# A hybrid attention and SSD layer on eight cores: the prologue's tables moved into a unit of their own, and the row copies one iteration later

## What is computed

```
proj = x @ w_in
q, k, v, f_logit, z_att, z_ssd, xbc, dt_raw = split(proj)
log_f = log_sigmoid(f_logit + b_forget);  F = cumsum(log_f)          # per head, over tokens
att = softmax(q.k / sqrt(128) + F[t] - F[s], causal) @ v * silu(z_att)
xbc = silu(causal_depthwise_conv(xbc, conv_w, conv_b))               # 4 taps
dt = softplus(dt_raw + dt_bias);  a_cs = cumsum(dt * A)              # within chunks of 128 tokens
m = (C.B^T) * exp(a_cs[l] - a_cs[s]);  y = m @ (x * dt) + C.state * exp(a_cs) + d_skip * x
state <- state * exp(a_cs[end]) + B^T @ (x * dt * exp(a_cs[end] - a_cs))
y = group_rmsnorm(y * silu(z_ssd)) * ssd_norm_w
out = layer_norm(alpha * x + concat[att, y] @ w_out)
```

## Time and profile before

| | us |
|---|---|
| median of 3 runs (lowest, highest) | 1702.08 (1698.3, 1717.66) |
| profiled execution, its time | 1711.28 |
| its span on the slowest core (core 1) | 1709.7 |
| spans of the eight cores | 1682.9 to 1709.7 |
| DVE, ACT, POOL busy in the span | 1138.4, 857.6, 866.2 |

### The profile page before, as it was taken

How to read it: one execution, slowest core, us unless ns; L and a number is a source line. 1 busy time by engine, 2 the same in 40 slices (tenths; PEclk the granted TensorE clock), 3 DMA queues, 4 the chain that set the end, 5 groups by cost and what they waited for, 6 DMA issues and landing times.

```text
span 1709.7 us, 31962 instructions; the slowest of 8 cores (1682.9 to 1709.7 us)
## 1 busy us (share of the span) xinstructions
PE 1644.7 (96%) x9108; PEld 803.3 (47%) x9108; DVE 1138.4 (67%) x2341; ACT 857.6 (50%) x1979; POOL 866.2 (51%) x1379
## 2 busy tenths in 40 slices
PE   6999889999999999999999999999899999999997
PEld 2444445554454445544544454454445544444443
DVE  2567657777776887787768677767677665444444
ACT  2767656665566666666665665666566620000000
POOL 3265555655565666565655555556566533222221
PEclk9999989999999999999999999999999999999999
DMA  9976783382248224522642373139465876544421
GB/s 150 152 102 118 120 124 86 78 145 63 56 86 131 63 70 98 116 71 63 123 82 64 75 131 71 54 75 141 98 122 113 185 197 199 138 139 136 135 93 74
DMA packets 180218, 185.30 MB, mean 108 GB/s; under 512 B 118668, under 2 KB 136844, under 8 KB 175820
## 3 DMA queue, kind: packets, MB, share of 16 engines
q1 hardware_dynamic: 162620, 120.07, 29.3%
q0 software_dynamic: 17424, 63.18, 23.3%
HBM read 193.50 MB, written 34.60 MB: 133 GB/s over the span
## 4 chain that ended last, share of the span: by engine, by line
PE 84%; DMA 10%; issue 2%; DVE 1%; ACT 1%; POOL 1%; SPq 0%; DVEq 0%; ACTq 0%; another core or an unknown queue 0%; POOLq 0%
PE bank L536 84%; DMA rowb<-arowd 4%; DMA btok<-BT 3%; DMA xq<-xT 3%; DMA slab<-w_out 1%; DMA xtok<-xsf 0%; ACT L547 0%; DVE acc L569 0%; ACT dec L547 0%; POOL xq L597 0%; POOL slab L597 0%; DVE BT L569 0%; DVE xt L569 0%; DVE xsf L569 0%; SPq L595 0%
## 5 line engine op out<-in xcount | busy, mean ns | idle before, releaser
L536 PE MATMUL bank<-xq,slab 128*128 128x512 bf16 x3072 | 731.8, 381 | 5.3 <-DMA slab<-wpack 2.7
L536 PE MATMUL bank<-slab,xq 128*128 128x512 bf16 x2048 | 482.1, 380 | 0.6 <-DMA slab<-wpack 0.6
L536 PEld LDWEIGHTS bank<-xq,slab 128*128 128x128 bf16 x3072 | 293.3, 98 | 312.5 <-issue 15.2
L569 DVE SCALAR_TENSOR_TENSOR acc<-u,cst,acc 128x512 f32<-128x512 f32 x384 | 317.6, 832 | 40.0 <-ACT acc L547 18.5
L536 PEld LDWEIGHTS bank<-slab,xq 128*128 128x128 bf16 x2048 | 198.3, 98 | 215.0 <-issue 3.2
L547 ACT ACTIVATE dec<-rowb,nb 128x128 bf16<-128x128 f32 x512 | 201.8, 397 | 48.5 <-PE bank L536 26.6
L547 ACT ACT_TABLE_LOAD x18 | 23.1, 1283 | 316.5 <-DVE mv L1135 308.7
L547 ACT ACTIVATE P<-bank,boff 128x512 bf16<-128x512 f32 x192 | 131.2, 683 | 78.0 <-PE bank L536 76.8
L536 PE MATMUL bank<-wo,mTa 128*128 128x512 bf16 x704 | 163.4, 379 | 0.0
L558 POOL TENSOR_TENSOR xdd<-xtok,dtde 128x256 bf16<-128x256 bf16 x120 | 82.9, 693 | 128.7 <-PE bank L536 85.9
L569 DVE SCALAR_TENSOR_TENSOR xt<-xt,bank 128x512 f32<-128x512 f32 x64 | 43.8, 685 | 138.5 <-PE bank L536 138.3
(11 more groups left out here) (108 smaller groups left out, 2245.6 us busy)
## 6 DMA issues: line engine op xcount, KB each, us to landing
slab<-wpack POOLq DMA_DIRECT2D x80, 512.0 KB, 7.4
rowb<-arowd SPq DMA_DIRECT2D x128, 256.0 KB, 3.5
xt<-x_tok SPq DMA_DIRECT2D x16, 1024.0 KB, 5.6
out<-xt SPq DMA_DIRECT2D x15, 1024.0 KB, 4.0
xq<-xT POOLq DMA_DIRECT2D x16, 512.0 KB, 26.5
gbc<-growd SPq DMA_DIRECT2D x32, 256.0 KB, 4.1
mixd<-yn SPq DMA_DIRECT2D x128, 64.0 KB, 2.0
slab<-w_out POOLq DMA_DIRECT2D x13, 512.0 KB, 10.4
```

Of the source, the lines that this page charges most:

```text
L536: fns.append(lambda e, o=o, a=a, b=b, s=s, t=t: e.matmul(o, a, b, start=s, stop=t))
L569: return p.op("dve", [lambda e: e.scalar_tensor_tensor(out=o, in0=a, scalar=s, in1=b, op0=op0, op1=op1)], dve_us(n, nptr) + (0.12 if nptr ...
```

## The change

The table part of `prologue_quarter` becomes a function of its own, `prologue_tables`, and a unit of its own, "tab". It is registered behind xs1 of the same step (behind xs1 of quarter 0 and behind B of quarter 1 in the opening list), takes no due time of its own, and its transposes and its matmul write two banks of the projection rotation instead of `PV0` and `PV1`. Iteration 1 reads the one copy of the rows, as iteration 0 does, and the row copies are made in iteration 1, behind the store of its attention output.

```diff
     def copies(i, q):
-        return (slice(0, 1), [1, 128, 512], b_row1[q]) if i == 0 else (slice(0, 16), [16, 8, 512], b_row[q])
+        return (slice(0, 1), [1, 128, 512], b_row1[q]) if i < 2 else (slice(0, 16), [16, 8, 512], b_row[q])
...
+    def prologue_tables(q, t):
+        sp_, e_, cs = [x[:, :] for x in tmps]
+        bs, be, bc = b_pt
+        pr = t - 40
+        B1 = PROJ[pi[0] % 3]
+        B2 = PROJ[(pi[0] + 1) % 3]
+        pi[0] += 2
         lst = []
...
-            fns.append(lambda e, c=c, o=o, src=src: e.transpose(banks[PV0][:, c * 128 + o:c * 128 + o + 64],
+            fns.append(lambda e, c=c, o=o, src=src: e.transpose(banks[B1][:, c * 128 + o:c * 128 + o + 64],
                                                                 src[:, c * 128:(c + 1) * 128], idn[0:64, 0:64]))
-        p.op("pe", fns, 0.6, [bc, bs, b_idn], [bkb[PV0]], pr, tail=0.2)
-        CPY("dve", tokt[:, :, :].rearrange("p a b -> p (a b)"), banks[PV0][:, :], 512, [bkb[PV0]], [b_tokt], pr)
-        MMS([(banks[PV1][:, 0:256], idn[:, 128:256], tokt[:, :, 0:64], True, True, 256, True)], [b_tokt, b_idn],
-            [bkb[PV1]], pr)
+        p.op("pe", fns, 0.6, [bc, bs, b_idn], [bkb[B1]], pr, tail=0.2)
+        CPY("dve", tokt[:, :, :].rearrange("p a b -> p (a b)"), banks[B1][:, :], 512, [bkb[B1]], [b_tokt], pr)
+        MMS([(banks[B2][:, 0:256], idn[:, 128:256], tokt[:, :, 0:64], True, True, 256, True)], [b_tokt, b_idn],
+            [bkb[B2]], pr)
...
-    first = [("fdt", 0), ("k", 0), ("xs0", 0), ("q", 0), ("xs1", 0), ("k", 1), ("xs0", 1), ("q", 1), ("fdt", 1),
-             ("xs1", 1), ("B", 0), ("B", 1), ("C", 0), ("C", 1)]
+    first = [("fdt", 0), ("k", 0), ("xs0", 0), ("q", 0), ("xs1", 0), ("tab", 0), ("k", 1), ("xs0", 1), ("q", 1),
+             ("fdt", 1), ("xs1", 1), ("B", 0), ("B", 1), ("tab", 1), ("C", 0), ("C", 1)]
...
-        do_unit(kind, q, 0, q, due())
+        do_unit(kind, q, 0, q, due() if kind != "tab" else T[0])
...
-                kinds = ["fdt"] + kinds
+                kinds = ["fdt"] + kinds[:4] + ["tab"] + kinds[4:]
...
-                t = due()
+                t = due() if kind != "tab" else T[0]
...
-        if i == 0:
-            copy_rows(q, T[0] + 40, b_mix_att[0][q])
+        if i == 1:
+            copy_rows(q, T[0] + 40, b_mix_att[1][q])
```

More of the change, by code:

```diff
@@ L732, in prologue_quarter @@
         for (c, o, src) in lst:
-            fns.append(lambda e, c=c, o=o, src=src: e.transpose(banks[PV0][:, c * 128 + o:c * 128 + o + 64],
+            fns.append(lambda e, c=c, o=o, src=src: e.transpose(banks[B1][:, c * 128 + o:c * 128 + o + 64],
                                                                 src[:, c * 128:(c + 1) * 128], idn[0:64, 0:64]))
-        p.op("pe", fns, 0.6, [bc, bs, b_idn], [bkb[PV0]], pr, tail=0.2)
-        CPY("dve", tokt[:, :, :].rearrange("p a b -> p (a b)"), banks[PV0][:, :], 512, [bkb[PV0]], [b_tokt], pr)
-        MMS([(banks[PV1][:, 0:256], idn[:, 128:256], tokt[:, :, 0:64], True, True, 256, True)], [b_tokt, b_idn],
-            [bkb[PV1]], pr)
-        ae = banks[PV1][:, 0:256].rearrange("p (c w) -> p c w", w=64)
+        p.op("pe", fns, 0.6, [bc, bs, b_idn], [bkb[B1]], pr, tail=0.2)
+        CPY("dve", tokt[:, :, :].rearrange("p a b -> p (a b)"), banks[B1][:, :], 512, [bkb[B1]], [b_tokt], pr)
+        MMS([(banks[B2][:, 0:256], idn[:, 128:256], tokt[:, :, 0:64], True, True, 256, True)], [b_tokt, b_idn],
+            [bkb[B2]], pr)
+        ae = banks[B2][:, 0:256].rearrange("p (c w) -> p c w", w=64)
         cs_ = slice(4 * q, 4 * q + 4)
@@ L744, in prologue_quarter @@
         CPY("dve", G_tok[:, cs_, :], tokt[:, :, 0:8], 32, [b_tokt], [bt], pr)
-        ACT(cd[:, cs_, :], ae[:, :, 32:64], AF.Exp, 128, [bkb[PV1]], [bt], pr)
+        ACT(cd[:, cs_, :], ae[:, :, 32:64], AF.Exp, 128, [bkb[B2]], [bt], pr)
         if q < 3:
-            CPY("dve", gref[:, q + 1, :], ae[:, 3, 0:8], 8, [bkb[PV1]], [b_tab[q + 1]], pr)
-        TT("dve", tmp2[:, :, :], ae[:, :, 32:64], at_, ALU.subtract, 128, [bkb[PV1], b_tokt], [b_tmp2], pr)
+            CPY("dve", gref[:, q + 1, :], ae[:, 3, 0:8], 8, [bkb[B2]], [b_tab[q + 1]], pr)
+        TT("dve", tmp2[:, :, :], ae[:, :, 32:64], at_, ALU.subtract, 128, [bkb[B2], b_tokt], [b_tmp2], pr)
         ACT(tmp2[:, :, :], tmp2[:, :, :], AF.Exp, 128, [], [b_tmp2], pr)
@@ L813, in do_unit @@
             prologue_quarter(q, t)
+        elif kind == "tab":
+            prologue_tables(q, t)
         elif kind in ("xs0", "xs1", "B", "C"):
```

## The result

The changed kernel took 1718.94 us (median of 14 runs, 1711.11 to 1954.13) where the kernel before took 1706.88 beside it (14 runs, 1698.3 to 1960.52): ratio 1.0063, 95% interval 1.0041 to 1.0085, some 10.7 us slower. In that last comparison, on another chip, the changed kernel was run once more and was at 1.0004 (0.9962 to 1.0046); there its runs had a mean of 1714.7 us, near the 1718.3 of the first time, while those of the kernel before, 1706.8 in the first comparison and 1706.5 to 1708.1 in the four between, were spread from 1702 to 1727 with a mean of 1714.0. So the first ratio is the better one.

A forecast was written before the change was run, and what follows sets the result against it. PE, busy 1644.7 of 1709.7 us, was taken as the bound, with waits behind late row loads. −12.9 + 1.3 + 0 + 5.5 = −6.1 us, off the median 1702.08, gave 1696 us, range 1684 to 1713.

The forecast's parts named there:

- rival (b): Wait returns in iteration 1, twice: two copies among slab loads or ahead of btok, 10.9 us each; +10.2, 1712 us; chance 0.16.
- rival (a): All gain: new copies cost nothing; −11.6 us, up to −18.0 with the mask waits, 1685 to 1690 us; chance 0.2.
- The gain (−12.9): Copies leaving iteration 0 save PE 2.8 us on the carry, 7.6 on exponential P, 2.5 on the clock, before 260 us.
- the signs named for being right: Included no rowb load over 15 us from 150 to 240 us, and PE near full from 225 to 250, clock 1.00.
- The first sign named for being wrong: A PE wait of over 8 us between 300 and 430 us.
- The tables' banks (+1.3): Table units take two projection banks, so the unit behind waits for ACT to empty one: 1.3 us, bounds 0 to 5.4.
- Rival (c): Tables still come late or the fourth load stays slow; only the carry's 2.8 us go: 1699 to 1702 us; chance 0.12.
- One-copy reads in iteration 1 (0, at most 3): Twenty loads read one copy, 0.7 us dearer each; 0 for PE, bounds 0 to 3 us.
- The copies in iteration 1 (+5.5, at quarter 2's place only): Quarter 2's copy, near 369 us among slab loads, delays btok: 0 to 10.9 us, middle 5.5 taken.
- rival (b)'s rule: Ring order on SP's queue: every SP transpose waits for the whole copy ahead of it.
- The planner's shifts: A plan made anew shifts later waits by a few us either way; counted only in the width of the range.

## Why the prediction was wrong

Forecast: 1696 us, 6 faster, in a range of 1684 to 1713. Measured: 1718.94 us, above it, and 0.63% slower than the kernel before beside it. On the median of the forecast that is 1702.08 × 1.0063 = 1712.8, the sum of rival (b). That the sum fits is luck: rival (b) charges two copies at 10.9 us each, and the loss came from the one-copy reads, from copies at other places and from the new order. (The −18.0 in rival (a) leaves out the banks' 1.3; its 1685 goes by −16.7.)

**The gain (−12.9)** was nearly right in size: 9.5 us on the mean core, with the masks' wait gone too, which I had kept (3.0 us before, 0.7 after on the mean core), and 3.1 us of a new one for CT, which I had not seen. The reason was half wrong: tables that come 23 us earlier gave 1.5 to 5.7 us alone, the missing copies 8.3 alone. One of the signs named for being right failed: on each of the eight cores of the changed kernel a row load issued at 181 to 183 us took 17.8 to 20.5 us, with no copy under way. On the core shown, 180 to 184 us:

```profile
rowb<-arowd SPq DMA_DIRECT2D x1, 256.0 KB, 20.5
```

So a load can get as long as that with no copy ahead of it. PE's wait for its reader, dec, was only 0.7 us on the mean core. The first sign named for being wrong did not show: the longest wait of PE from 300 to 450 us was 5.3 us, and the loss came in several short ones.

**The tables' banks (+1.3)**: no wait on the transposes shows in the changed kernel. Rival (c) falls, too: they do come early.

**One-copy reads in iteration 1 (0, at most 3)** is the first step that failed. I priced them from quiet rows, 4.9 against 4.2 us. Alone among slab loads it was 10.1 against 5.8 (10.4 against 7.6 with the real rows), and at unchanged order 3.6 us of the mean core with one-row copies, 5.8 with full ones. The earlier trace rows had the warning: the load of 179.61 took 13.91 us with no copy ahead of it, among slab loads, and I had put it down to the slabs alone.

**The copies in iteration 1 (+5.5, at quarter 2's place only)** is the second. 4.5 us of the mean core was measured with sixteen-row reads and 6.7 with one-copy reads, so the size was near, but by luck, since the place was not the one priced. I had taken 9.4 us, the quiet copy of the earlier trace rows, for three of the four. In the changed kernel, issued at 260 to 300 and 300 to 330 us, the big transfers of the first two took

```profile
arowd<-arowd SPq DMA_DIRECT2D x1, 960.0 KB, 19.8
...
arowd<-arowd SPq DMA_DIRECT2D x1, 960.0 KB, 14.5
```

and row loads there took twice as long as with one-row copies, 8.3 against 4.0 us from 300 to 330. Quarter 2's, which I had feared, was issued at 390 on the core shown, after the jam, and landed in 8.1 us (371 to 384 and 8.6 to 19.8 on the others). PE did wait there for an xtok that landed right behind the copy, on seven of the eight cores, as I had feared of btok, but 1.5 us on the mean core, 3.3 on the one shown. So rival (b)'s rule held, and its place was the small one.

The trace has that rule on all eight cores. Of 129 transfers that were issued on SP's queue in the changed kernel while the big transfer of an earlier copy was under way, none landed before it; the closest came 0.2 us after it. The load issued at 274.18, behind the copy of 271.60 that took 19.8 us, landed 0.6 us after it (issues from 274 to 274.5 us):

```profile
rowb<-arowd SPq DMA_DIRECT2D x1, 256.0 KB, 17.8
```

The 25 row loads from 262 to 330 us with a copy under way ahead of them took 10.4 us, the other 25 took 6.4, and with one-row copies it was 4.0: a load pays most where it stands behind a copy. That is the ring order of the Trainium skill ("DMA: Bandwidth & Descriptors", Queues, rings and completion order), which I had made rival (b)'s reason. The same section of the Trainium skill says that an engine takes turns between the queues that have work for it, a packet at a time. The row loads that took 10.1 us beside slab loads on the other queue, with no copy ahead, agree with that.

**The planner's shifts**, which I counted "in the width" alone, are the third: the btok behind four w_out loads, 4.6 us of waiting on the mean core in a stretch that lost 6.5 more, and at least 2.6 us for gz at 400 to 450 us in the changed kernel and in the four that keep its order, whatever their transfers.

By the table of losses: −9.5 + 11.6 (300–450) + 2.9 (500–600) + 6.5 (1200–1368) − 2.6 (1000–1200) = +8.9, against +10.3 for the whole stretch to 1500 us. Left open: why four copies in iteration 1 lost 19.5 us; why the slowest core's distance from the mean changes from kernel to kernel; and what of the new order, other than btok's place and gz, costs the rest. Which planner input to mend was not tried: it counts 1.3 us for a row load, from one copy or sixteen.

## What to carry over

Price a read where it will stand: a load that repeats one row from DRAM was nearly as quick as one from sixteen in a quiet stretch (3.8 against 3.2 us, 4.0 against 3.5) and a third to three quarters slower among weight loads (10.4 against 7.6, 10.1 against 5.8). Moving a transfer out of a jam gains what the jam cost and pays again where it lands, so look at every place that it gets, not only the worst, and take the price from a row with the same neighbours. Where a planner fixes the order, an edit can remake it all the way to the end: test causes with the order held and the transfers changed, and look in the last iteration for what has changed sides with a weight load. Where the metric is the slowest of several cores, compare the mean core too: here it showed a loss that the slowest core hid in one comparison, and showed a gain to be no gain.

## What the chip showed unexpectedly

At equal bytes a row load's source decides how it shares: beside two to three slab loads a core, 256 KB from one copy landed in 10.1 us (21 loads, median of the cores' medians) and from sixteen rows of another tensor in 5.8 (23 loads), with no large copies under way in either; from 300 to 330 us, with fewer slab loads, 4.0 and 3.5. With the real rows and the same order it was 10.4 and 7.6. The slab loads beside them did not gain from it (8.2 us each). A transfer from DRAM to DRAM of 960 KB that took 9.4 us in one place took 19.8 and 14.5 in others without many slab loads. On SP's queue nothing landed before a copy that was ahead of it, 129 times of 129. And SP's stands of 2.9 to 11.6 us at one wait, with the loads queued behind it, cost nothing that could be measured in the kernel with one-row copies.
